# First inputs in single tiles, second scores of the first attention pass in spare banks, gates ahead of a weight split

## The reference

```
h = concat(meta_tokens, x)                       # 272 x 2048
# layer 0, mixer A: sliding-window attention, 32 heads of 64, 4 key/value heads
q, k, v, gate = split(h @ w_in_a)
s = q k^T * 64**-0.5 + bias_table[bucket(distance)]    # masked to the window
p = softmax(concat(s, sink))
y = ((p @ v) * silu(gate)) @ w_out_a
h = layer_norm(alpha * h + y)
# layer 1, mixer B: stick-breaking attention, 16 heads of 128
q, k, v, gate = split(h @ w_in_b)
w = exp(z - suffix_sums(softplus(z)))
y = ((w @ v) * silu(gate)) @ w_out_b
out = layer_norm(alpha * h + y)[16:]
```

## Time and profile before

| | |
|---|---|
| median of 3 runs | 933.26 us (931.73 to 933.75) |
| profiled execution's own time | 933.26 us |
| span of its profile, first to last instruction | 931.4 us |
| PE busy | 908.1 us (98%) |
| DVE, ACT, POOL busy | 548.8, 429.0, 63.4 us |
| mean granted clock of TensorE | 0.991 of full |
| HBM traffic | 153 MB, mean 164 GB/s |

### The profile page before, as it was taken

How to read it: one execution, slowest core, us unless ns; L and a number is a source line. 1 busy time by engine, 2 the same in 40 slices (tenths; PEclk the granted TensorE clock), 3 DMA queues, 4 the chain that set the end, 5 groups by cost and what they waited for, 6 DMA issues and landing times.

```text
span 931.4 us, 18753 instructions
## 1 busy us (share of the span) xinstructions
PE 908.1 (98%) x7596; PEld 892.4 (96%) x7596; DVE 548.8 (59%) x709; ACT 429.0 (46%) x668; POOL 63.4 (7%) x85
## 2 busy tenths in 40 slices
PE   7999999999999999999899999999999999999995
PEld 7998999999999999999899999999999999999995
DVE  6367677667765766675645455464636455545556
ACT  6456555455555333475443353534444443453320
POOL 1050233033110000000000000000000000000000
PEclk8999999999999999999999999999999999999998
DMA  9565654465443545324444453434343434454422
GB/s 348 187 168 191 210 173 127 148 204 172 127 153 120 181 181 181 136 84 170 168 173 143 167 180 135 172 144 180 135 180 135 171 144 158 158 213 177 190 99 90
DMA packets 24674, 153.04 MB, mean 164 GB/s; under 512 B 3344, under 2 KB 3360, under 8 KB 8128
## 3 DMA queue, kind: packets, MB, share of 16 engines
q1 hardware_dynamic: 21312, 142.19, 42.0%
q0 software_dynamic: 2896, 7.70, 4.0%
q10 hardware_dynamic: 432, 2.65, 0.8%
HBM read 150.35 MB, written 2.18 MB: 164 GB/s over the span
## 4 chain that ended last, share of the span: by engine, by line
PE 85%; DVE 5%; issue 4%; DMA 4%; POOL 1%; ACT 1%; SPq 1%; DVEq 0%; POOLq 0%
PE bank L275 72%; PE bank L602 2%; PE bank L406 2%; PE bank L366 2%; DMA raw<-chunks 1%; DMA work<-chunks 1%; DVE w_lo L889 1%; PE bank L478 1%; DVE work L941 1%; PE bank L514 1%; DMA work<-bias_table 1%; PE bank L492 1%; PE bank L542 0%; PE bank L479 0%; PE bank L544 0%
## 5 line engine op out<-in xcount | busy, mean ns | idle before, releaser
L275 PE MATMUL bank<-x_hi,w_hi 128*128 128x272 f32 (+1 forms) x1472 | 425.7, 289 | 2.5 <-DVE work L1207 2.5
L275 PE MATMUL bank<-x_lo,w_hi 128*128 128x272 f32 (+1 forms) x1472 | 422.3, 287 | 0.0
L275 PE MATMUL bank<-x_hi,w_lo 128*128 128x272 f32 (+1 forms) x1472 | 422.0, 287 | 0.0
L889 DVE TENSOR_TENSOR w_lo<-raw,w_hi 128x2048 fp32r<-128x2048 f32 x127 | 292.5, 2310 | 202.5 <-ACT w_hi L624 202.2
L624 ACT ACTIVATE w_hi<-raw 128x2048 fp32r<-128x2048 f32 x128 | 244.3, 1911 | 198.3 <-PE bank L275 119.8
L275 PEld LDWEIGHTS bank<-x_hi,w_hi 128*128 128x128 f32 x1472 | 278.2, 189 | 3.7 <-issue 3.0
L275 PEld LDWEIGHTS bank<-x_hi,w_lo 128*128 128x128 f32 x1472 | 278.0, 189 | 0.0
L275 PEld LDWEIGHTS bank<-x_lo,w_hi 128*128 128x128 f32 x1472 | 277.6, 189 | 0.0
L275 PE MATMUL bank<-og_hi,w_hi 128*128 128x272 f32 x256 | 74.9, 293 | 0.3 <-DVE og_lo L987 0.3
L275 PE MATMUL bank<-og_hi,w_lo 128*128 128x272 f32 x256 | 74.1, 289 | 0.0
L275 PE MATMUL bank<-og_lo,w_hi 128*128 128x272 f32 x256 | 73.7, 288 | 0.0
(11 more groups left out here) (208 smaller groups left out, 1111.4 us busy)
## 6 DMA issues: line engine op xcount, KB each, us to landing
raw<-chunks SPq DMA_DIRECT2D x128, 1024.0 KB, 4.8
work<-bias_table POOLq DMA_DIRECT2D x8, 512.0 KB, 5.6
work<-chunks SPq DMA_DIRECT2D x4, 512.0 KB, 12.6
work<-bias_table POOLq DMA_DIRECT2D x8, 256.0 KB, 6.6
work<-ln_rows ACTq DMA_DIRECT2D x1, 2048.0 KB, 7.5
out<-work SPq DMA_DIRECT2D x8, 256.0 KB, 2.4
h<-xT SPq DMA_DIRECT2D x3, 544.0 KB, 9.8
raw<-chunks SPq DMA_DIRECT2D x3, 512.0 KB, 8.6
```

Of the source, the lines that this page charges most:

```text
L275: last = mm(o, l, r, start=(kt == 0 and n == 0), stop=(kt == KT - 1 and n == 2))
L889: V.tensor_tensor(w_lo[:, slot, :, :], raw[:, half, :, :], w_hi[:, slot, :, :].bitcast(f32), ALU.subtract).then_inc(lo_ready, 1)
```

## The change

It has four parts.

1. The input's first part of two tiles becomes two parts of one tile; ACT issues three input parts instead of two. Weight parts that arrive as two tiles (2-3, 4-5, 6-7) are still loaded as before, but ACT and DVE split them tile by tile, and PE waits tile by tile. SP's waits for the raw slots name the same tiles as before by the new counts.
2. `SPINS_0` goes from 15 to 19.
3. In pass 0 of attention A the scores of heads 2 and 3 go to banks 6 and 7, which held the bias table's sums until DVE had read them (`tab_ready`); the wait for `scores_read` goes.
4. In the first iteration of B, `split_hi(P + 5, 0)` stands behind the gates' exponentials on ACT, and `split_lo(P + 5, 0)` behind the gates' operations on DVE, ahead of `split_lo(P + 5, 1)`.

```diff
-SPINS_0 = 15
+SPINS_0 = 19
...
+        def scores_at(i, c):
+            return bank[6:8] if isinstance(i, int) and i == 0 and c >= 2 else scores
...
-        X_PARTS = ((0, 2), (2, 4), (4, 8), (8, 12), (12, 16))
-        X_A, X_EARLY = len(X_PARTS), 2
+        X_PARTS = ((0, 1), (1, 2), (2, 4), (4, 8), (8, 12), (12, 16))
+        X_A, X_EARLY = len(X_PARTS), 3
...
-        KV_ORDER = [[0, 1], [2], [3, 4], [5], [6, 7, 8]]
+        KV_ORDER = [[0], [1], [2], [3, 4], [5], [6, 7, 8]]
...
             if n < len(KV_PARTS):
                 lo, hi = KV_PARTS[n]
-                r = kv_raw[:, lo:hi, :, :]
-                h, l = (w[:, 0:2, lo:hi, :].rearrange("p s k c -> p k s c") for w in (w_hi, w_lo))
-                return r, h, l
+                return [(kv_raw[:, k, :, :],) + tuple(w[:, 0:2, k, :] for w in (w_hi, w_lo)) for k in range(lo, hi)]
...
             for s in range(RAW_SLOTS):
-                sp.wait_ge(kv_lo, (3, 5)[s])
+                sp.wait_ge(kv_lo, (4, 8)[s])
...
                 x_arrived(k)
-                if k in [lo for lo, _ in KV_PARTS]:
-                    pe.wait_ge(kv_lo, [lo for lo, _ in KV_PARTS].index(k) + 1)
+                pe.wait_ge(kv_lo, k + 1)
...
-                if u or not (isinstance(i, int) and i == 0):
+                banks = scores_at(i, 2 * u)
+                if not (isinstance(i, int) and i == 0):
                     pe.wait_ge(scores_read, 2 * (4 * i + 2 * u))
+                elif u:
+                    pe.wait_ge(tab_ready, 2)
...
# ACT, body_b
                 if isinstance(i, int):
                     split_hi(P + 4, 1)
-                    split_hi(P + 5, 0)
                 for u in range(2):
                     act.wait_ge(tile_full[u], P + 3 + 1)
                     A(b["gate"][:, u, :], acc[u][:, 0:SEQ], ACT.Exp, scale=-1.0).then_inc(gateb_exp, 1)
+                if isinstance(i, int):
+                    split_hi(P + 5, 0)
                 split_hi(P + 5, 1)
...
# DVE, body_b
                 split_lo(P + 4, 1)
-                split_lo(P + 5, 0)
+                if not isinstance(i, int):
+                    split_lo(P + 5, 0)
                 for u in range(2):
                     dve.wait_ge(gateb_exp, 2 * i + u + 1)
...
+                if isinstance(i, int):
+                    split_lo(P + 5, 0)
                 split_lo(P + 5, 1)
```

More of the change, by code:

```diff
@@ L145, in trunk @@
         tile_free = [sem("tile_free0"), sem("tile_free1")]
-        x_loaded = [sem(f"x_loaded{n}") for n in range(5)]
+        x_loaded = [sem(f"x_loaded{n}") for n in range(6)]
         kv_loaded = [sem(f"kv_loaded{n}") for n in range(9)]
@@ L195, in kv_views, with kv_step @@
                 lo, hi = KV_PARTS[n]
-                r = kv_raw[:, lo:hi, :, :]
-                h, l = (w[:, 0:2, lo:hi, :].rearrange("p s k c -> p k s c") for w in (w_hi, w_lo))
-                return r, h, l
+                return [(kv_raw[:, k, :, :],) + tuple(w[:, 0:2, k, :] for w in (w_hi, w_lo)) for k in range(lo, hi)]
             chunk, lo, hi = KV_1_PARTS[n - len(KV_PARTS)]
-            return kv_1_raw[chunk][:, lo:hi, :], w_hi[:, chunk, lo:hi, :], w_lo[:, chunk, lo:hi, :]
+            return [(kv_1_raw[chunk][:, lo:hi, :], w_hi[:, chunk, lo:hi, :], w_lo[:, chunk, lo:hi, :])]
+        def kv_step(n):
+            return KV_PARTS[n][0] if n < len(KV_PARTS) else HALF + n - len(KV_PARTS)
         @block.sync
@@ L315, in _ @@
                 if k % 4 == 0:
-                    pe.wait_ge(kv_lo, len(KV_PARTS) + 1 + k // 4)
+                    pe.wait_ge(kv_lo, HALF + 1 + k // 4)
                 for u in range(2):
@@ L324, in _ @@
                     if u == 0 and k % 4 == 0:
-                        pe.wait_ge(kv_lo, len(KV_PARTS) + 3 + k // 4)
+                        pe.wait_ge(kv_lo, HALF + 3 + k // 4)
                     last = first_terms(3, u, k)
@@ L365, in scores_of @@
                             part = slice(64 * h2, 64 * h2 + 64)
-                            m = mm(scores[h2][0:rows, lo:lo + n], q[part, u, q_cut], k[part, 0:n],
+                            m = mm(banks[h2][0:rows, lo:lo + n], q[part, u, q_cut], k[part, 0:n],
                                    start=(step == 0), stop=(step == 2))
@@ L644, in kv_part_hi @@
                 act.wait_ge(kv_loaded[n], 16)
-                r, h_part, _ = kv_views(n)
-                A(h_part, r, ACT.Copy).then_inc(kv_hi, 1)
+                for r, h_part, _ in kv_views(n):
+                    A(h_part, r, ACT.Copy).then_inc(kv_hi, 1)
             for n in range(X_A):
@@ L902, in kv_part_lo @@
                 dve.wait_ge(kv_loaded[n], 16)
-                dve.wait_ge(kv_hi, n + 1)
-                r, h_part, l_part = kv_views(n)
-                V.tensor_tensor(l_part, r, h_part.bitcast(f32), ALU.subtract).then_inc(kv_lo, 1)
+                for m, (r, h_part, l_part) in enumerate(kv_views(n)):
+                    dve.wait_ge(kv_hi, kv_step(n) + m + 1)
+                    V.tensor_tensor(l_part, r, h_part.bitcast(f32), ALU.subtract).then_inc(kv_lo, 1)
             for n in range(X_A):
@@ L910, in _ @@
                     kv_part_lo(m)
-            dve.wait_ge(kv_lo, 9)
+            dve.wait_ge(kv_lo, HALF + 4)
             V.memset(a["VL_cur"], 0.0).then_inc(banks_cleared, 1)
@@ L940, in row_maxima @@
                     dve.wait_ge(scores_ready, 4 * i + c + 1)
-                    V.tensor_tensor(a["t"][:, c, 0:416], scores[c % 2][:, 0:416], a["bias"][:, c, 0:416],
+                    V.tensor_tensor(a["t"][:, c, 0:416], scores_at(i, c)[c % 2][:, 0:416], a["bias"][:, c, 0:416],
                                     ALU.add).then_inc(scores_read, 1)
-                    V.tensor_tensor(a["t"][0:16, c, 416:432], scores[c % 2][0:16, 416:432],
+                    V.tensor_tensor(a["t"][0:16, c, 416:432], scores_at(i, c)[c % 2][0:16, 416:432],
                                     a["bias"][0:16, c, 416:432], ALU.add).then_inc(scores_read, 1)
```

## The result

The changed kernel takes 927.11 us at the median of its 4 runs (926.44 to 927.36), the kernel before 932.97 beside it (4 runs, 931.73 to 933.75): a ratio of 0.9941 with a 95% interval of 0.9928 to 0.9955. The forecast was 926.2 with a range of 924.4 to 928.6. In the profiled execution the time is 926.44 and the span 924.0, with a mean granted clock of 0.996 where it was 0.991.

What follows compares the result with a forecast made beforehand. PE, busy 98% of the span, was taken as the bound, leaving its waits and half-clock stretches. Start 0.85, clock 1.75, second scores 1.2 and gates 3.3 sum to 7.1 us: 933.26 to 926.2 us, range 924.4 to 928.6.

Steps and rivals of the forecast that it cites:

- the likeliest case: The prediction's own forecast for the whole kernel: 926.2 us, own range 924.9 to 927.6, chance 0.60.
- What bounds the kernel: PE works 98% of the span, so only its idle time and stretches at half clock can give time back.
- The start: PE's first real matmul: smaller input part lands before the weights, so PE starts 0.85 us earlier, bounds 0 and 1.2.
- The stall, costed at nothing: Split pieces at the start just fit at tile 4; cost nothing, or one PE stall of 0.3 us if transfers are late.
- The clock at the start: More spins shorten PE's idle time before the first matmul to 1.9 us; 1.75 us gained, bounds 0 and 2.6.
- The rival with this clock lost: At the start as many matmuls still run at half clock: 928.0 us, chance 0.14.
- The second scores: Attention A, pass 0: spare banks remove PE's 1.33 us wait before the second scores; 1.2 us gained.
- The rival that this gain is absorbed: The second scores' gain is lost at the transpose that already waits 0.5 us: 927.4 us, chance 0.06.
- The gates: First gates of B: 2.45 us of wait and 1.35 of slow clock saved, 0.5 new wait; net 3.3 us.
- The rival with more given back: Gates of B: the late load costs 1.3 us instead of 0.5, and some more at P+5; 927.2 to 928, chance 0.10.
- The weight stream falls behind: B's remaining seven rounds: the 4.8 us delay is not caught up, 18 us slower, 944 us; chance 0.02.
- Outside the span: Time of the execution not in the span, 1.86 us in the profiled execution before the change.

Runs made afterwards that it cites:

- the fastest version: Changed kernel with tiles 2 and 3 of the input and of the weights also as transfers of one tile each: median 925.92 us, ratio 0.9926.

## Why the prediction was right, by its own steps

The sum was 7.1 us. The same two profiled executions give 7.4 of span and 6.8 of time; the mean over all executions gives 6.0 and 5.6. The measured median is 0.9 above 926.2, inside the likeliest case's own range. The gain itself was put too high: 7.1 us against 5.9 between the medians, a ratio of 0.9924 where the interval begins at 0.9928.

- **What bounds the kernel** held: all of the gain comes from PE's idle time and clock, and each named wait went or shrank. Taking one part out costs 0.8 (tiles), 0.6 (spins), 1.2 (scores) and 3.3 us (gates) in the mean time, 5.9 together, near the whole of 5.6. Only the gates' cost is far beyond its standard error; the other three have 0.4 to 0.6.
- **The start**, 0.85 earlier: 1.59 was measured. The bound of 1.2 was too near. With the smaller input parts the first weights landed 1.4 us sooner, where the bound allowed 0.3. The weights are then no longer last: ACT waits for the input part until 5.14 and takes the weights right behind it, at 5.47. ACT's input parts of one tile have rows of 1,088 bytes where they had 2,176. The Trainium skill (DMA: Bandwidth & Descriptors, Queues, rings and completion order) says that each DMA engine goes round the queues that have work, one packet at a time; a queue with smaller packets would then leave more of each round to the other. The trace agrees as far as it goes: ACT's 0.56 MB went in 288 packets before and in 432 now, and the landings are 5.4 and 4.0 us. No run here changes the row size alone, so it may be the fewer bytes ahead of the weights as well.
- **The stall, costed at nothing**: this step failed. It looked at tile 4, and the stall came at tile 2, at 1.18 us between two matmuls (1.0 idle): the two-tile part became the third in the queue and took 7.3 us. The prediction's "PE stalls 0.3 once" has the mechanism and not the size. The version with tiles 2 and 3 in parts of their own has no such stall and ends the projections 1.0 us sooner.
- **The clock at the start**, 1.75: 2.3 measured. The clock did not drop, which the prediction priced at 2.6; but 24 matmuls at full clock took 3.14 us, 0.131 each and not 0.12, so 5.48 - 3.14 = 2.34. PE idled only 1.0 us, not 1.9, since it started earlier than thought and the 38 records took 4.87 us. The rival with this clock lost was real in other kernels: with 15 spins it fell behind 1.78 us. 1.59 + 2.34 - 1.18 = 2.75, the lead of 2.7 at the end of the first two projections; 0.85 + 1.75 = 2.6 was predicted. Two terms put too low and a stall put at nothing made this sum come out right: the agreement here is luck.
- **The second scores**, 1.2: the lead grows from 2.7 at the first scores (55.57 to 52.84) to 4.1, by 1.4; taking the part out costs 1.2 in the mean time. The transposes' wait kept its 0.5. The rival that this gain is absorbed may be right in part, at another place: at the value matmuls behind ACT's split, where the wait was 0.25 before, 0.78 with this part alone and 1.0 in the fastest version. In the two profiles of the changed kernel it was 0.24 and 0.66, so it is not the same in each execution.
- **The gates**, 3.3: 3.5 (lead 4.0 to 7.5), with a new wait of 0.36 where 0.5 was said, at the place and of the kind named. The clock stayed at 1.00. The rival with more given back is seen once, 0.9 us with the gates alone. This term is the best shown. From the first to the last matmul of B's attention it is 378.1 to 378.6 us in the profiles of the kernel before and of its four variants with the old order, 379.3 in the changed kernel with the old order, and 374.5 to 375.2 in all eight with the new order. Behind it 106.2 to 106.3 us follow in every profile.
- **The weight stream falls behind** did not happen: no wait on a split recurs in B, and the lead of 7.5 stands to the end.
- **Outside the span**, held constant at 1.86: 2.44 in the profiled execution, 2.35 on average against 1.89. This step failed by 0.5 us and accounts for half of the 0.9 by which the median is over the forecast.

What is left is the difference between a pair and the means. The profiled execution of before (931.4) is 0.7 us above its mean and that of the changed kernel (924.0) is 0.7 below its own, so the gain read from this pair overstates the mean gain by 1.4. The reason for a scatter of 5 us before is shown in part. Its profile has idle times of 3.7, 1.3 and 2.5 us in three places (the one at the scores is 1.2 to 2.0 in its relatives), and the profiles of its relatives differ in whether the clock fell at the start and at the scores. Its mean granted clock goes with the span: in the 29 executions with 0.992 or less the mean span is 931.9, in the 31 with more it is 929.6. The Trainium skill (TensorE: Matmul & The Clock Gate, part 1) says that the count of slow matmuls at a kernel's start varies between runs of one kernel. No kernel here has two profiles with a drop, so its count is not compared. What the runs show is that the scatter goes with the long idle times: the changed kernel, with none over 1.4 us in its two profiles, scatters by 1.1 us over 8 executions, and the kernel before by 5.4 over 60.

One thing stays open. Added alone, the parts gain 1.5, 0.2, 0.4 and 1.0 us, 3.1 together with a standard error of some 1.3 (all four are set against the same mean of the kernel before), and all at once 5.6, so a part of the difference may be scatter. Part of the difference is shown: a gain ahead of a transfer with its own date is in part lost there (the gates' wait of 3.7 us with the other three parts), and a longer wait brings a drop of the clock with it (1.57 us at the scores). The stretch of B's attention narrows it further. With the gates alone, and in the changed kernel with the old order:

```profile
L514 PE MATMUL bank<-work x32: 377/378/463, 448.0 to 823.2; 128*128 128x256 f32 x32
...
L523 PE MATMUL bank<-work x32: 377/378/463, 443.1 to 822.4; 128*128 128x256 f32 x32
```

The same reordering is worth 378.1 - 375.2 = 2.9 us on the kernel before and 379.3 - 374.6 = 4.7 us in the changed one, so the two are worth more together than apart. The new wait lies inside this stretch, so it does not explain why the gates alone gain 1.0 us in the mean; that would have to come from the part ahead of B, where this profile is 0.9 us later than that of the kernel before with the same code (448.0 against 447.1), or from executions that were not profiled. This stays open.

## What to carry to other kernels

When PE is busy 98% of the time, list its waits together with the clock behind each. A wait behind which the clock falls costs more than itself: here 2.3 us beside the 3.7 at the start and about 1.4 beside the 2.5 at the gates. Shortening it to 1 us at the start, and removing it at the gates, gave back both. Parts of such a change are not additive: a gain may last only until the next transfer with its own date, so ask for each step what arrives no earlier, and check both engines that have it in their order. And compare means over many executions when a single one scatters by 5 us: one profiled pair gave 7.4 where the mean gave 6.0.

## What the runs showed of the hardware that was not expected

- **Idle time and clock.** Of the idle times of PE read in the profiles here, those up to 1.36 us were not followed by a drop (among them 1.00, 1.01, 1.20, 1.25, 1.33 and 1.36). Between 1.57 and 2.19 both occur: a drop behind 1.57, 1.78, 2.0, 2.0 and 2.19, none behind 1.59, 1.8 and 2.07. From 2.4 on there was always one (2.4 to 3.8, eleven cases). Length alone does not decide in between. The drop need not come at once: behind 1.57 and 1.78 us the clock fell more than 1 us after PE had gone on.
- **Small input parts beside the weights.** With ACT's first input parts at half their size SP's first weight part landed after 4.0 to 4.3 us (eight profiles) instead of 5.4 to 5.8 (six), while the two-tile input part, where it was third, took 7.3 to 8.2 us.
- **One more transfer issued by ACT at the start** goes with some 0.3 us more outside the span on average (2.22 against 1.91, as the only edit).
